# Blocks of 64 rows in place of masked products over 128 in the RWKV stage of a one-core decoder trunk

## The reference

```
def step(S, inp):
    r_t, w_t, k_t, v_t, kk_t, a_t = inp
    sa = jnp.einsum('bhij,bhj->bhi', S, -kk_t)
    S = (S * w_t[:, :, None, :] + sa[..., None] * (kk_t * a_t)[:, :, None, :]
         + v_t[..., None] * k_t[:, :, None, :])
    return S, jnp.einsum('bhij,bhj->bhi', S, r_t)
```

## Time and profile before

| | |
|---|---|
| runs, median (lowest to highest) | 3560.51 us (3560.0 to 3560.63) |
| the profiled execution: its own time, its span | 3560.32 us, 3558.6 us |
| PE, PEld busy | 3362.0 us (94%), 2682.7 us (75%) |
| DVE, ACT, POOL busy | 955.1 us (27%), 463.6 us (13%), 600.5 us (17%) |
| mean granted TensorE clock | 0.970 |
| moved by DMA | 335.27 MB, mean 94 GB/s |

### The profile page before, as it was taken

How to read it: one execution, slowest core, us unless ns; L and a number is a source line. 1 busy time by engine, 2 the same in 40 slices (tenths; PEclk the granted TensorE clock), 3 DMA queues, 4 the chain that set the end, 5 groups by cost and what they waited for, 6 DMA issues and landing times.

```text
span 3558.6 us, 39904 instructions
## 1 busy us (share of the span) xinstructions
PE 3362.0 (94%) x16700; PEld 2682.7 (75%) x16700; DVE 955.1 (27%) x1950; ACT 463.6 (13%) x778; POOL 600.5 (17%) x613
## 2 busy tenths in 40 slices
PE   6999998979999989999989999898799999899999
PEld 4777776657888778888857777775588877688887
DVE  3222002344333223331032220123343432333300
ACT  2001003302111111000010000123031101100000
POOL 3333000320000013440023320002200000144300
PEclk8999999989999999999989999999899999999999
DMA  6343332331110222213153433323311112122121
GB/s 265 142 153 115 121 120 75 125 98 50 45 45 30 78 83 71 83 60 105 62 213 142 155 118 113 124 82 97 98 47 45 45 45 75 71 83 83 56 82 66
DMA packets 61711, 335.27 MB, mean 94 GB/s; under 512 B 10592, under 2 KB 10976, under 8 KB 32480
## 3 DMA queue, kind: packets, MB, share of 16 engines
q1 hardware_dynamic: 46656, 295.40, 22.5%
q0 software_dynamic: 12320, 33.57, 3.1%
q10 hardware_dynamic: 2560, 3.80, 0.3%
HBM read 326.71 MB, written 6.02 MB: 94 GB/s over the span
## 4 chain that ended last, share of the span: by engine, by line
PE 86%; issue 3%; ACT 3%; DVE 3%; DMA 2%; POOLq 2%; POOL 1%; SPq 0%; DVEq 0%; ACTq 0%
PE ps L544 85%; DMA ring<-w_ada 2%; POOLq L514 1%; ACT ws L1125 1%; ACT u L1125 1%; DMA ws<-cache 1%; POOL ws L516 1%; DVE ws L1360 1%; ACT L1125 1%; DVE y L1360 0%; POOLq L516 0%; PE ps L954 0%; DVE proj L1360 0%; DVE ws L1764 0%; DVE x L1363 0%
## 5 line engine op out<-in xcount | busy, mean ns | idle before, releaser
L544 PE MATMUL ps<-u,ring 128*128 128x272 f32 x4864 | 1210.4, 400 | 57.4 <-ACT u L1125 51.1
L544 PEld LDWEIGHTS ps<-u,ring 128*128 128x128 f32 x4864 | 918.7, 193 | 283.1 <-ACT u L1125 53.8
L544 PE MATMUL ps<-proj,ring 128*128 128x272 f32 x3328 | 771.2, 394 | 9.4 <-DVE proj L1360 9.4
L544 PEld LDWEIGHTS ps<-proj,ring 128*128 128x128 f32 x3328 | 632.9, 191 | 146.9 <-DVE proj L1360 12.0
L1360 DVE TENSOR_TENSOR ws<-ws,ps 128x272 f32<-128x272 f32 (+3 forms) x570 | 269.3, 476 | 1167.1 <-PE ps L544 1158.3
L528 POOL TENSOR_TENSOR masked_room<-ring 128x512 f32<-128x512 f32 x44 | 55.8, 1267 | 1590.4 <-DMA ring<-w_up 1361.1
L544 PE MATMUL ps<-y,ring 128*128 128x272 f32 x1216 | 312.4, 393 | 0.5 <-DVE proj L1360 0.5
L1125 ACT ACTIVATE ws<-ps 128x272 f32<-128x272 f32 (+5 forms) x374 | 163.1, 443 | 1056.2 <-PE ps L544 974.3
L516 POOL DMA_DIRECT2D ws<-cache x256 | 137.5, 537 | 828.6 <-issue 828.6
L544 PEld LDWEIGHTS ps<-y,ring 128*128 128x128 f32 x1216 | 231.4, 191 | 49.8 <-DVE proj L1360 2.0
L544 PE MATMUL ps<-y,masked_room 128*128 128x272 f32 x1056 | 258.4, 395 | 0.3 <-DVE y L1360 0.2
(11 more groups left out here) (191 smaller groups left out, 1910.2 us busy)
## 6 DMA issues: line engine op xcount, KB each, us to landing
ring<-w_up SPq DMA_DIRECT2D x88, 1024.0 KB, 4.8
ring<-w_ada SPq DMA_DIRECT2D x72, 1024.0 KB, 5.3
ring<-w_down SPq DMA_DIRECT2D x64, 704.0 KB, 4.1
ws<-cache POOLq DMA_DIRECT2D x256, 128.0 KB, 2.3
ring<-w_gate SPq DMA_DIRECT2D x32, 1024.0 KB, 4.8
ring<-w_in SPq DMA_DIRECT2D x22, 1024.0 KB, 4.9
ring<-w_branch SPq DMA_DIRECT2D x32, 256.0 KB, 4.6
ring<-w_out SPq DMA_DIRECT2D x8, 1024.0 KB, 5.0
```

What stands on the lines that cost most here:

```text
L544: return nc.tensor.matmul(out, lhsT, rhs, start=start, stop=stop, skip_group_check=skip)
```

## The change

The four matrices for both chunks are kept as `[128, 4, 64]`: rows 0 to 63 hold chunk 0, rows 64 to 127 chunk 1, 64 columns for each head, and nothing of the two zero quarters. Products are 64 rows by 64 columns. Three helpers replace `heads`:

- `by_chunk`: for each head and chunk, rows of the chunk in, partitions of the chunk out (8 products in one bank).
- `by_channel`: for products over channels, the 64 rows of the head in, the partitions of the chunk out; the two heads of a feature tile go to two banks, b and b+1 (8 products).
- `turn_chunks`: a transpose as a product with a 64x64 identity (8 products in place of 4 transposes).

Heads then stand in the order 0, 2, 1, 3, which `slot(h)` gives. The padded copies and their memsets are gone, DVE's and ACT's work on the matrices is 256 columns wide in place of 512, and the constants are 320 columns narrower (1,280 bytes a partition). The output products use the two row halves apart and write to banks 6 and 7. In the sample stage, `small` and `by_seq` go over the head's 64 rows in place of 128 rows with zeros. All in all:

```
-(IDENT, ONES, BLK, TRI, CAUS, CNEG, M16U, M16L, E32L, E64L, SU64, LE64) = [P * i for i in range(12)]
-S4U = 12 * P
+(IDENT, ONES, BLK, TRI, CAUS, CNEG) = [P * i for i in range(6)]
+(M16U, M16L, E32L, E64L, SU64, LE64, ID64) = [6 * P + CH * i for i in range(7)]
+S4U = 6 * P + 7 * CH
...
-        AtP, at = carve(at, 4, P)
-        RtP, at = carve(at, 4, P)
-        BtP, at = carve(at, 4, P)
         mat0 = at
-        MA, at = carve(at, 4, P)
+        MA, at = carve(at, 4, CH)
...
-                def heads(b, lhsT, rhs, n=P, rows=P):
+                def by_chunk(b, lhsT, rhs):
 
                     for h in range(NH):
-                        m = mm(ps[0:rows, b, h * n:h * n + n], lhsT(h), rhs(h))
+                        for c in range(2):
+                            rows = slice(CH * c, CH * c + CH)
+                            m = mm(ps[rows, b, h * CH:h * CH + CH], lhsT[rows, h, :], rhs[rows, h, :])
                     return m
+                def by_channel(b, n, lhsT, rhs):
+
+                    for ft in range(2):
+                        for c in range(2):
+                            for q in range(2):
+                                r, rows, at = slice(HD * q, HD * q + HD), slice(CH * c, CH * c + CH), n * P + ft * CH
+                                m = mm(ps[rows, b + q, at:at + CH], lhsT[r, ft, rows], rhs[r, ft, rows])
+                    return m
+
+                def turn_chunks(b, v):
+                    for h in range(NH):
+                        for c in range(2):
+                            rows = slice(CH * c, CH * c + CH)
+                            m = mm(ps[rows, b, h * CH:h * CH + CH], v[rows, h, :],
+                                   cst[rows, IDENT + CH * c:IDENT + CH * c + CH])
+                    return m
...
-                    heads(0, ft_of(Bt), hd_of(AtP))
-                    heads(1, ft_of(At), hd_of(BtP)).then_inc(rw_pe.sem, 1)
-                    heads(2, ft_of(Kt_), hd_of(AtP))
-                    heads(3, ft_of(Bt), hd_of(RtP))
+                    by_channel(0, 0, Bt, At)
+                    by_channel(0, 1, At, Bt).then_inc(rw_pe.sem, 1)
+                    by_channel(2, 0, Kt_, At)
+                    by_channel(2, 1, Bt, Rt)
...
-                        heads(0, hd_of(ET), hd_of(xa))
-                        for h in range(NH):
-                            m = nc.tensor.transpose(ps[:, 1, h * P:h * P + P], xa[:, h, :], cmat(IDENT))
-                        m.then_inc(rw_pe.sem, 1)
+                        by_chunk(0, ET, xa)
+                        turn_chunks(1, xa).then_inc(rw_pe.sem, 1)
...
-                                mm(ps[rows, 0, h * HD:h * HD + HD], LakT[:, h, rows],
-                                   vt[:, h * HD:h * HD + HD], start=h % 2 == 0, stop=False, skip=True)
+                                mm(ps[rows, 0, h * HD:h * HD + HD], LakT[rows, slot(h), :],
+                                   vt[rows, h * HD:h * HD + HD], start=h % 2 == 0, stop=False, skip=True)
                             m = mm(ps[rows, 0, ft * P:ft * P + P], At[:, ft, rows], sbd[:, ft, :],
                                    start=False, skip=True)
...
-                for v in (AtP, RtP, BtP):
-                    V.memset(v[:, :, :], 0.0)
...
-                for o, i in ((AtP, At), (RtP, Rt), (BtP, Bt)):
-                    o = o.rearrange("p (f q) n -> p f q n", f=2)
-                    for q in range(2):
-                        r = slice(64 * q, 64 * q + 64)
-                        m = V.tensor_copy(o[r, :, q, 0:n], i[r, :, 0:n])
```

More of the change, by code:

```diff
@@ L928, in _ @@
                     pe_.wait_ge(rw_dve.sem, tile_dve(2))
-                    heads(0, hd_of(MB), hd_of(MA))
-                    heads(1, hd_of(MA), hd_of(MB)).then_inc(rw_pe.sem, 1)
+                    by_chunk(0, MB, MA)
+                    by_chunk(1, MA, MB).then_inc(rw_pe.sem, 1)
                     piece(1)
@@ L933, in _ @@
                     pe_.wait_ge(rw_dve.sem, tile_dve(3))
[L934 to L936 removed]
+                    by_chunk(0, MD, ME)
+                    by_chunk(1, MD, MC)
+                    by_chunk(7, MC, MD).then_inc(rw_pe.sem, 1)
                     piece(2)
@@ L939, in _ @@
                     pe_.wait_ge(rw_dve.sem, tile_dve(4))
-                    heads(0, hd_of(MB), hd_of(MF))
-                    heads(3, ft_of(Kt_), hd_of(RtP))
-                    heads(1, hd_of(MA), hd_of(MB)).then_inc(rw_pe.sem, 1)
+                    by_chunk(0, MB, MF)
+                    by_channel(2, 1, Kt_, Rt)
+                    by_chunk(1, MA, MB).then_inc(rw_pe.sem, 1)
                     piece(3)
@@ L945, in _ @@
                     pe_.wait_ge(rw_dve.sem, tile_dve(5))
-                    heads(0, hd_of(MC), hd_of(ME)).then_inc(rw_pe.sem, 1)
+                    by_chunk(0, MC, ME).then_inc(rw_pe.sem, 1)
                     piece(4)
@@ L972, in _ @@
                         for ft in range(2):
-                            mm(ps[:, 6, 256 + ft * P + q0:256 + ft * P + q0 + CH], sbd[:, ft, :], Rt[:, ft, rows],
-                               start=c == 0 and ft == 0, stop=False, skip=True)
+                            mm(ps[:, 6 + c, 256 + ft * CH:256 + ft * CH + CH], sbd[:, ft, :], Rt[:, ft, rows],
+                               start=ft == 0, stop=False, skip=True)
                         piece(9 + 3 * c)
@@ L990, in _ @@
                             piece(11)
[L991 to L996, removed]
+                    for v, w in ((sat, MrbT), (vt, MrkT)):
+                        for h in range(NH):
+                            ft, po = h // 2, HD * (h % 2)
+                            for c in range(2):
+                                rows, at = slice(CH * c, CH * c + CH), 256 + ft * CH
+                                m = mm(ps[po:po + HD, 6 + c, at:at + CH], v[rows, h * HD:h * HD + HD],
+                                       w[rows, slot(h), :], start=False, stop=v is vt, skip=True)
                     m.then_inc(rw_pe.sem, 1)
@@ L1033, in by_seq @@
                             m = mm(ps[po:po + HD, b, ft * TS + s * TD:ft * TS + s * TD + TD],
-                                   lp[:, SWKV + (ft * NSEQ + s) * HD:SWKV + (ft * NSEQ + s) * HD + HD],
-                                   rhs[:, h, s * TD:s * TD + TD], start=first and h < 2 and s == 0,
+                                   lp[po:po + HD, SWKV + (ft * NSEQ + s) * HD:SWKV + (ft * NSEQ + s) * HD + HD],
+                                   rhs[po:po + HD, ft, s * TD:s * TD + TD], start=first and h < 2 and s == 0,
                                    stop=False, skip=True)
                     return m
-                by_seq(1, AtP, True)
+                by_seq(1, At, True)
                 for h in range(NH):
@@ L1042, in _ @@
                     m = mm(ps[po:po + HD, 1, ft * TS:ft * TS + TS], vt[0:TS, h * HD:h * HD + HD],
-                           LakT[0:TS, h, 0:TS], start=False, skip=True)
+                           LakT[0:TS, slot(h), 0:TS], start=False, skip=True)
                 m.then_inc(rs_pe.sem, 1)
```

147 lines of the change are left out of this document (77 added, 70 removed).

## The result

The changed kernel takes **3516.31 us**, the median of 4 runs (3514.54 to 3518.06), against 3560.57 us for the kernel before in the same session (3560.0 to 3562.07, 4 runs). The ratio is 0.9875, 95% interval 0.9858 to 0.9892: 1.2% faster, 44 us. The prediction said 3516.

The account below looks back on a forecast made before the run. PE was taken to bound the kernel, 86% of the span. Eight tiles at 5.3 us gave 42 us, with sample stage and constants 43.9, so 3560.3 - 43.9 = 3516 us; range 3500 to 3548.

Parts of the forecast that it names:

- Removed and added records: Per tile on PE: 144 full-array records removed, 16.06 us; quarter-size products added in two or four streams, 7.66 us.
- A visit: PE going to another weight shape and back to full-array work: 0.34 us each, nine a tile, 3.06 us added.
- Shape changes in the chunk loop: Three shape changes inside a chunk-loop group, about 0.09, 0.14 and 0.09 us, twice a tile: 0.64 us added.
- Output products: 32 output-product records a tile in four quarters, 0.46 us against about 0.93: 0.47 us saved.
- The wait at a tile's start: PE's wait at a tile's start goes with six DVE copies: 0.9 us over the kernel, 0.1 a tile saved.
- Sum of a tile: Per tile, 16.06 - 7.66 - 3.06 - 0.64 + 0.47 + 0.1 = 5.3 us saved; 42 us over eight tiles.
- Outside the tiles: Sample stage's first records in two row halves save 0.55 us a layer, 1.1 in all; smaller constants save 0.4.
- a shared bank forbids overlap: Rival: row halves writing into one PSUM bank in `by_chunk` and `turn_chunks` do not overlap; 3568 us, slower; 9% chance.
- Nothing overlaps: Rival: no 64x64 products overlap, `by_channel` and output products included; 3607 us; 4% chance.
- four quarters as two: Rival: four quarters run as two streams in `by_channel` and the output products; 3529 us; 8% chance.
- Other prices for visits: Rival: weight-shape visits cost other than 0.34 us; twice gives 3545 us (5%), none 3487 (cheaper case 4%, say 3500).
- The clock stays at 1.00: Rival judged here: granted clock falls in the tiles' lighter groups, 3.4 us a tile lost, 3543 us; 5% chance.

Follow-up runs that it names:

- Experiment 1: Changed kernel with the two loops of `by_chunk` and `turn_chunks` exchanged, all of rows 0 to 63 first: 3540.27 us.
- Experiment 3: Changed kernel with an unread one-column product put into each of 14 groups a tile: full-array 3563.66 us, 64x64 quarter 3527.41 us (one run each).
- Experiment 5: Changed kernel with each chunk's `LakT` products before its `At` products, 3512.22 us; or with both chunks' `LakT` products moved into the last 64x64 matrix group, 3503.04 us.
- experiment 4: Changed kernel with six unread padded copies a tile put back on DVE ahead of the first groups: 3515.38 us.
- lak_first: Changed kernel with the four `LakT` products of each chunk ahead of the two `At` products: 3512.22 us.
- lak_state: Changed kernel with both chunks' `LakT` products moved into the last 64x64 matrix group, plus the edit of `state_blocks`: 3497.5 us.
- state_blocks: Changed kernel with each chunk's four 64x128 new-state products made eight of 64x64, alternating between column halves: 3506.9 us.

## Why the prediction was right

Mechanism, sign and size held. Two terms of a tile were mis-sized, the chunk loop's changes of shape and the wait, and it is luck that their errors offset one another in part. Term by term of a tile, against the rows above:

- **Removed and added records (16.06 less 7.66).** Held. The price of 0.058 a step with two or four quarters at work is seen in `by_chunk` and in `by_channel`; both unknowns, one bank and four quarters at once, came out as fully side by side. Experiment 1 takes not quite half of the overlap in `by_chunk` away and loses 23 us.
- **A visit, 0.34.** Held. In the trace, group C at 935.56 was due at 935.47 (0.09 in); its 48 records are 24 steps, 1.39, and take 1.55 (0.16); the piece behind group D has six records that take 1.47 in place of 1.37 (0.10): 0.35. Summed over the nine visits of the tile, the part of the distances between starts that exceeds those among like records comes to 3.07, against 3.06. Experiment 3 shows that the cause is the change of shape, with 0.24 for those parts of a visit that it has.
- **Shape changes in the chunk loop, 0.64.** The term that was too small. A chunk's products up to `ws,rtail` took 1.05 us before (972.05 to 973.10) and take 1.47 now: 0.42, 0.84 for both chunks, in place of 0.64. I had priced the changes between small shapes by the gaps at full-array work, halves of a visit; there are three, and each costs about 0.14. Experiment 5 takes two of three away and gains 0.28 a chunk, 0.14 each.
- **Output products, 0.47.** 0.62 us now (979.49 to 980.11) against 1.07: 0.45.
- **The wait at a tile's start, 0.1.** It is gone from the list of waits, and this term was too small as well. PE's timeline of the kernel before:

```profile
995.72 1.08 PE L544 MATMUL ps<-y,ring 128*128 128x272 f32 x4
997.01 3.84 PE L544 MATMUL ps<-ws 128*128 128x128 f32 x32 [0.21 <-DVE ws L1764]
```

Four records of 272 columns step by 0.229, so the group was due at 996.64 and started 0.37 late: it waited for the six copies, which end at 996.96 (a row of DVE at 995.17, 1.79 long). The list of waits counts only the 0.21 in which no record ran any more; the time that PE loses is the distance between starts. And the first distance behind the wait is 0.10 longer than in a group that runs on (its 32 records take 3.67 us to the transposes at 1000.68; the layer's first group, which waits for nothing, takes 3.57, from 872.49 to 876.06). Together 0.48 in the tiles with a wait, two a layer. Besides, experiment 4 shows that left on DVE beside the faster PE the six copies would cost 3 to 4 us.

- **Sum of a tile: 5.3 forecast, 5.40 measured.** With what was measured (144 records without a wait are 16.04): 16.04 - 7.66 - 3.07 - 0.84 + 0.45 + 0.48 = 5.40, and nothing is left over for the narrower work of DVE and ACT. The chunk loop cost 0.20 more than its term, the wait gave 0.38 more. Where there was no such wait a tile gained less, so the eight come to 41.5 us, for 42.
- **Outside the tiles.** The small products at the sample stage's start now take 0.75 us (the row at 1099.08 to the transposes at 1099.83) for 1.38: 0.63 gained where 0.55 was due, 1.3 for two layers. From the pieces ahead of its first tile to these transposes a layer is 21.4 us shorter: 20.8 for the tiles and 0.6 for this. The constants are within the 0.6 us by which the start-up is shorter. Tiles, sample stage and start-up are 43.4 of the 45.8 us between the profiled executions; the sum said 43.9. The other 2.4 I put down to the low-clock stretches (3.2 in the two windows above, less what others lose), for which the sum has nothing. The measured tiles and the rest are 0.5 under the sum, the clock 2.4 over it, and the profiled execution lies 1.8 under its median: these nearly cancel. So the mechanism holds within a few us, and that the total came within 1 us of the forecast is luck.

The rivals: the first (a shared bank forbids overlap, 3568) falls with the pairs at 931.99 and with experiment 1, which would have cost nothing if the halves had not overlapped. "Nothing overlaps" and "four quarters as two" fall with the four starts in 0.02 us. Other prices for visits fall with the timeline, where all nine of a tile are seen; experiment 3 alone would not settle the size, and it inserts nothing into a group that begins with `by_channel`. "Nothing but semaphore waits" as the cause of the price falls with experiment 3. The clock stays at 1.00 in the tile.

Where did the gain come from, then? Quartering removes 8.4 us of records a tile and pays 3.9 of it back at the borders between shapes. Of those 3.9, `lak_first` recovers 0.56 by order alone; joining groups and cutting the neighbours to the same blocks brings another 1.8 in `lak_state`, but 0.86 of that is the state's own products running in two streams (0.43 a chunk) and no border.

## What to carry to other kernels

When products of half-size blocks replace masked full ones, count two things from the trace: steps, which fall by the number of halves or quarters of the array that work side by side, and visits, at 0.34 us each here. A lone group of 16 records hardly pays (0.46 + 0.34 against 0.89 for the eight records of the four full products before); so join groups of one shape, move strays of a shape into the group that already has it, and cut neighbours to the same shape even where their own count of records does not fall. Let halves alternate within two products. And compare variants by the distance between two equal rows of the repeated stage when the difference is a few us, since the clock in other stages moves the total by as much.

## What the hardware showed that was not expected

- Records of different halves start out of program order: in `state_blocks` an output product starts at 977.92, ahead of state products at 977.96 and 978.07 that stand before it in the program. How far a half can go ahead has a bound here: two products (four records) may wait in front of a half at hardly any cost (0.027 us a group), four products may not (0.207).
- A change between two small shapes (64x64 and 128x64) costs about 0.14 us, not much less than half a visit of 0.34 to and from the full array.
- A wait that counts 0.21 us in the list of waits, behind records 0.39 us long that start every 0.23, cost 0.37 us of starts and 0.10 in the next distance.
- Stretches of low granted clock in code that was not touched moved with the kernel's length: PEclk of a 24-us window went from 0.64 to 0.79. Why they fall where they do no run here tells.
